# Block 1's attention in two score places: scores of two pairs in three PSUM banks each, turns in pieces through one bank, heads copied by VectorE

## The chip, the cores and the metric

One core of a Trainium2 chip runs the whole program. The metric is the device time in microseconds (us) of one execution; the number given is the median of several. TensorE (PE) multiplies, VectorE (DVE) and ScalarE (ACT) work on what it leaves in PSUM, GpSimd (POOL) works on SBUF, SyncE (SP) starts the weight transfers. PSUM has eight banks of 512 float32 columns; BANK = 512 in the code. Each engine executes its own instructions in order and waits on semaphores for the others.

## The reference

Two transformer blocks run one after the other on 512 tokens of width 1024, each with two layers. The change touches only the attention of the first block. It has eight windowed heads with a sink logit (branch A, at most 384 near keys and 256 context keys) and eight full heads (branch B, all 512 + 256 keys):

```python
s_win = jnp.where(valid[None, :, None, None], s_win, NEG_INF)
s_ctx = jnp.einsum('bnqhgd,bchd->bnhgqc', qb, kc).astype(jnp.float32) * scale
p = softmax_with_sink(jnp.concatenate([s_win, s_ctx], axis=-1), sink.reshape(N_KV_A, G)).astype(v.dtype)
...
s = jnp.einsum('bqhgd,bkhd->bhgqk', qblk, kall).astype(jnp.float32) * scale
p = jax.nn.softmax(s, axis=-1).astype(vall.dtype)
return jnp.einsum('bhgqk,bkhd->bqhd', p, vall)
```

In layer 0 the 256 context tokens attend as well, each to the 256 context keys, in both branches (`context_attention`). Both blocks go on with projections and a gated MLP; all is float32.

## The kernel before

The program is a row of stages, each an `nc.Block()` with one instruction stream per engine; a stage begins when all engines have left the one before. Most of the time goes into matrix products in which each weight is split into a high part (ACT, line 456) and a low part (DVE, line 459). Block 1's attention is one such stage per layer: layer 0 from about 290 to 482 us, layer 1 from about 1375 to 1535 us. Most of the rest is the same before and after the change.

An attention stage walks over *pairs*: two heads (e = 0 and 1) of one tile of 128 queries. Head 0 uses the first 64 rows of TensorE, head 1 the last 64, so that the score products of both run side by side. `pairs1(l)` makes the list. For each of four head pairs and each of four query tiles stands first a windowed pair (branch A: 512, 640, 640, 512 keys for the four tiles, with a mask and a sink), then a full pair (branch B: 768 keys). That makes 32 pairs. Layer 0 adds 16 small pairs for the context tokens, of 256 keys, with and without sink in turn. In this text A512, A640 and B name the three large kinds, and "small" the fourth; a *group* is the eight pairs of one head pair, A512 B A640 B A640 B A512 B.

A pair takes these steps. The letters are those of the prediction:

- S, `scores` (PE, line 1533): the scores of both heads into PSUM.
- M, `maxima` (DVE, lines 1589 to 1597): for each head the mask (in place) and the row maximum, then a scaled copy of it, one 128x1 instruction.
- E, `exponent` (ACT, line 1636): exp into `probs`, one instruction per head; for a pair with sink two more of 128x1 (line 1643).
- N, `normalize` (DVE, lines 1605 to 1609): the reciprocal of the sums, and one multiplication per head over all keys.
- T, `turn` (PE, line 1549): transposes of `probs` into PSUM, 128x128 at a time.
- C, `copy` (ACT, line 1627): the transposed tiles back into `probs`.
- V, `values` (PE, line 1562): the product with the values, into the PSUM place `O_AT`.
- H, `heads` (ACT, line 1648): that result to SBUF; POOL then splits it (lines 1680 and 1681).

What sets the order is the code of the four loops. In turn i of the loop PE does S(i), T(i-1), V(i-2); DVE does N(i-1), M(i); ACT does E(i), C(i-1), H(i-2). A large pair of scores has one place in PSUM, banks 0 and 1 for head 0 and banks 2 and 3 for head 1, so S(i) waits for both E(i-1) (`clear_of`). Where two pairs in a row have at most 512 keys there are two places, and `begun` lets S and M run one pair ahead: PE then does S(i+1) before T(i-1). T has three banks, one after the other for the heads (`T_AT`). The last turns also split the first two weight units of the next stage (`split_unit`, one instruction of 128x1024 on ACT and one on DVE each).

## Time and profile before

| | us |
|---|---|
| median of 3 runs | 3474.71 (3474.41 to 3478.57) |
| the profiled execution | 3481.14 |
| its span, first to last instruction | 3479.2 |
| PE busy | 3310.0 (95%) |
| DVE busy | 1807.0 (52%) |
| ACT busy | 1210.4 (35%) |
| mean granted TensorE clock | 0.988 of 2.4 GHz |

The two attention stages together take about 350 us of the span. Busy time of PE counts the modelled ends of its matmuls, about 0.2 us of tail after the last one of a burst, so a PE that looks almost busy can still have room. A float32 matmul shows as two records in the trace, and a transpose as one. "Idle before" in a row is how long the engine stood before that instruction, and the name after the arrow is what it waited for.

### The profile page before, as it was taken

What the parts mean: (1) busy time and instruction counts of PE and PEld (TensorE: products, weight loads), DVE (VectorE), ACT (ScalarE), POOL (GpSimd) and SP (SyncE); (2) the same over time, 40 slices, a digit from 0 to 9 for tenths busy, and PEclk for the clock granted to TensorE, in tenths of its full rate; (3) what the DMA queues carried; (4) which work ended last, traced back from release to release, by engine and by line L of the source; (5) the groups of instructions that cost most, each with busy time, mean ns of one, the idle gap of its engine ahead of it and who ended that gap; (6) DMA issues with size and microseconds to landing.
All of it is one profiled execution on the core that took longest, in us unless ns stands there. A gap on an engine that the chain in (4) does not pass through costs nothing. (4 is left out here: it accounts for less than half of the span.)

```text
span 3479.2 us, 49806 instructions
## 1 busy us (share of the span) xinstructions
PE 3310.0 (95%) x20432; PEld 2653.7 (76%) x20432; DVE 1807.0 (52%) x2942; ACT 1210.4 (35%) x2054; POOL 445.8 (13%) x477
## 2 busy tenths in 40 slices
PE   6998899999999999889999999899999998899998
PEld 4887678788888787666787867667888777578886
DVE  5875767654232466765323357664443385734433
ACT  3214763311131222763223333353322332533322
POOL 0211111000000021113600133120000022200000
PEclk9999999999999999999999999999999999999999
DMA  6420013354212122012222321012223320022232
GB/s 241 146 103 14 1 45 130 120 197 146 65 63 73 49 86 72 1 37 88 97 92 96 103 85 62 20 43 91 97 91 103 103 85 3 31 91 97 91 102 80
DMA packets 78266, 290.67 MB, mean 84 GB/s; under 512 B 8672, under 2 KB 9056, under 8 KB 77280
## 3 DMA queue, kind: packets, MB, share of 16 engines
q1 hardware_dynamic: 78048, 287.55, 24.3%
q8 instruction: 163, 2.67, 0.3%
q14 instruction: 55, 0.45, 0.0%
HBM read 285.42 MB, written 2.10 MB: 83 GB/s over the span
## 5 line engine op out<-in xcount | busy, mean ns | idle before, releaser
L459 DVE TENSOR_TENSOR w_low<-ring,w_high 128x1024 fp32r<-128x1024 f32 x418 | 526.8, 1260 | 1350.8 <-ACT w_high L456 1350.1
L494 PE MATMUL ps<-arena_r,w_high 128*128 128x512 f32 x3568 | 1143.8, 386 | 10.4 <-PEq L1515 9.1
L456 ACT ACTIVATE w_high<-ring 128x1024 fp32r<-128x1024 f32 x418 | 442.9, 1060 | 1517.6 <-PE ps L494 1508.5
L494 PEld LDWEIGHTS ps<-arena_r,w_high 128*128 128x128 f32 x3568 | 646.8, 188 | 163.6 <-issue 16.9
L494 PE MATMUL ps<-low,w_high 128*128 128x512 f32 (+1 forms) x2448 | 765.2, 361 | 0.0
L494 PE MATMUL ps<-high,w_high 128*128 128x512 f32 x2368 | 737.1, 362 | 15.1 <-DVE low L992 6.9
L494 PE MATMUL ps<-high,w_low 128*128 128x512 f32 x2368 | 730.9, 359 | 0.0
L494 PE MATMUL ps<-arena_r,w_low 128*128 128x512 f32 (+1 forms) x1456 | 546.3, 388 | 0.0
L494 PEld LDWEIGHTS ps<-low,w_high 128*128 128x128 f32 x2448 | 412.1, 189 | 74.9 <-issue 1.2
L494 PEld LDWEIGHTS ps<-high,w_high 128*128 128x128 f32 x2368 | 395.4, 189 | 95.4 <-issue 12.0
L494 PEld LDWEIGHTS ps<-high,w_low 128*128 128x128 f32 x2368 | 395.1, 188 | 70.5
L494 PEld LDWEIGHTS ps<-arena_r,w_low 128*128 128x128 f32 x1456 | 267.1, 189 | 61.6
L555 POOL TENSOR_TENSOR tmp<-tmp 128x512 f32<-128x512 f32 (+1 forms) x42 | 67.3, 1603 | 1528.8 <-ACT tmp L545 1528.8
L1636 ACT ACTIVATE probs<-ps,stat 128x512 f32<-128x512 f32 (+3 forms) x224 | 153.6, 692 | 92.3 <-DVE stat L1594 46.8
L1533 PE MATMUL ps<-arena 64*128 64x256 f32 (+6 forms) x784 | 143.3, 438 | 44.4 <-ACT probs L1636 38.4
L1533 PEld LDWEIGHTS ps<-arena 64*128 64x128 f32 (+1 forms) x784 | 83.1, 193 | 87.3 <-ACT probs L1636 54.0
L1549 PE MATMUL ps<-const,probs 128*128 128x128 f32 x896 | 126.5, 285 | 17.9 <-DVE probs L1609 8.9
L1549 PEld LDWEIGHTS ps<-const,probs 128*128 128x128 f32 x896 | 100.8, 144 | 54.3 <-DVE probs L1609 42.0
L802 DVE CUSTOM_DVE_ANT_0 arena<-arena 128x1024 f32<-128x1024 f32 x104 | 137.1, 1362 | 0.0
L1627 ACT ACTIVATE probs<-ps 128x512 f32<-128x512 f32 (+3 forms) x224 | 121.1, 597 | 24.4 <-PE ps L1549 23.5
L494 PE MATMUL ps<-low,w_low 128*128 128x512 f32 x368 | 127.4, 374 | 0.0
L1562 PE MATMUL ps<-probs,arena 128*64 128x128 f32 x1792 | 123.5, 280 | 2.8 <-ACT hL L1648 2.2
(353 smaller groups left out, 2941.4 us busy)
## 6 DMA issues: line engine op xcount, KB each, us to landing
ring<-in_weights SPq DMA_DIRECT2D x428, 512.0 KB, 3.3
arena<-in_ada_rows SPq DMA_DIRECT2D x80, 512.0 KB, 3.9
arena<-in_ada SPq DMA_DIRECT2D x16, 512.0 KB, 15.7
arena<-in_cond_rows SPq DMA_DIRECT2D x3, 1024.0 KB, 5.9
xL<-in_x SPq DMA_DIRECT2D x1, 2048.0 KB, 10.4
out<-xL SPq DMA_DIRECT2D x4, 512.0 KB, 2.7
low_f<-in_low_rank SPq DMA_DIRECT2D x3, 512.0 KB, 4.3
const<-in_const SPq DMA_DIRECT2D x1, 1104.0 KB, 5.4
```

Of the source, the lines that this page charges most:

```text
L456: act.activation(w_high[:, slot, :], ring[:, place, :], ACT.Copy).then_inc(unit_high.sem, 1)
L459: dve.tensor_tensor(w_low[:, slot, :], ring[:, place, :], w_high[:, slot, :].bitcast(F32), ALU.subtract).then_inc(unit_free.sem, 1)
L494: mm = pe.matmul(bank(4 * (t % 2) + 2 * p + s, width), w, g.split[k][s][x], start=(n == 0 and m == 0), stop=(n == len(part) - 1 and m == 2))
L555: pool.tensor_tensor(tmp[:, 1, 0:total], tmp[:, 1, 0:total], tmp[:, 0, 0:total], ALU.add).then_inc(squares_sum.sem, 1)
L802: ins = dve.tensor_tensor_reduce(out, self.slots[place], self.vectors[s], 1.0, 0.0, ALU.mult, ALU.add, mod[:, to, s:s + 1])
L1533: mm = pe.matmul(ps[:, to:to + w], q, k, start=True, stop=True)
L1549: mm = pe.transpose(ps[:, to:to + P], probs[:, j % 3, e, m * P:m * P + P], con("ident"))
L1562: mm = pe.matmul(ps[e * HD:e * HD + HD, O_AT:O_AT + P], pair["values"][e][m], probs[:, j % 3, e, m * P:m * P + P], start=(m == 0 and not b ...
L1627: act.activation(probs[:, j % 3, e, 0:keys], ps[:, turned_at(j, e):turned_at(j, e) + keys], ACT.Copy).then_inc(turned_out.sem, 1)
L1636: act.activation(probs[:, i % 3, e, 0:keys], ps[:, scores_at(i, e):scores_at(i, e) + keys], ACT.Exp, bias=st[:, 2 + e:3 + e], scale=scale, ...
```

## The change

A second function, `attention_by_bank`, is added and is used for block 1 in both layers; `attention` stays for block 2. Six things differ from the function before:

- Scores have two places for every kind of pair: banks 0 to 2 and banks 3 to 5, in turn. A large pair has head 0 in the first bank and half of the second, head 1 in the other half and the third. S(i) waits for E(i-2).
- The middle bank of a large pair is shared by both heads. Head 1 writes it first and head 0 last, and between the two PE waits on its own semaphore (`shared_bank`). For B, head 1's scores are cut at 256 and not at 512, so the order is 512 (head 0), 256 (head 1), 512 (head 1), wait, 256 (head 0).
- The probabilities of both heads stand one behind the other, and T and C go through one bank (bank 6) in pieces of up to 512 columns: B and A640 have three pieces, A512 two, a small pair one. Each piece waits until the piece before it is copied.
- The order within a turn i of the loop is new. PE: T(i-1) piece 0, S(i+1), T(i-1) piece 1, V(i-2), T(i-1) piece 2. DVE: N(i-1), H(i-3), M(i+1). ACT: E(i) head 0, C(i-1) piece 0, E(i) head 1, C(i-1) piece 1, sinks, C(i-1) piece 2.
- H is done by DVE (`tensor_copy`), after N and before M, and in the last turns after the two `split_unit`.
- E of a large pair waits for the maxima of both heads.

```diff
+        shared_bank = count("shared_bank")
...
+        def attention_by_bank(pairs, scale, heads_on_vector=False):
+            n = len(pairs)
+            T_AT, O_AT = 6 * BANK, 7 * BANK
+            chunks = [-(-2 * pair["keys"] // BANK) for pair in pairs]
+            chunk0 = [sum(chunks[:i]) for i in range(n + 1)]
+            def scores_at(i, e):
+                return (i % 2) * 3 * BANK + e * (T if pairs[i]["keys"] > BANK else BANK)
...
+            def chunk(i, c):
+                return c * BANK, min((c + 1) * BANK, 2 * pairs[i]["keys"])
+                    def scores(i):
+                        pair = pairs[i]
+                        if i >= 2:
+                            pe.wait_ge(exp_out.sem, exp_out.at(2 * (i - 2) + 2))
+                        for c in range(len(pair["scores"][0])):
+                            for f in ((0, 1) if c % 2 == 0 else (1, 0)):
+                                q, k, at, w = pair["scores"][f][c]
+                                to = scores_at(i, f) + at
+                                shared = pair["keys"] > BANK and (f, c) == (0, len(pair["scores"][0]) - 1)
+                                if shared:
+                                    pe.wait_ge(shared_bank.sem, shared_bank.at(large(i + 1)))
+                                mm = pe.matmul(ps[:, to:to + w], q, k, start=True, stop=True)
+                                if pair["keys"] > BANK and (f, c) == (1, 0):
+                                    mm.then_inc(shared_bank.sem, 1)
+                        mm.then_inc(scores_in.sem, 2)
+                    def turn(j, c):
+                        first, end = chunk(j, c)
+                        pe.wait_ge(probs_out.sem, probs_out.at(2 * j + (1 if end <= pairs[j]["keys"] else 2)))
+                        if chunk0[j] + c:
+                            pe.wait_ge(turned_out.sem, turned_out.at(chunk0[j] + c))
+                        for at in range(first, end, P):
+                            to = T_AT + at - first
+                            mm = pe.transpose(ps[:, to:to + P], flat(j)[:, at:at + P], con("ident"))
+                        mm.then_inc(turned_in.sem, 1)
+                    def values(j):
+                        pair = pairs[j]
+                        pe.wait_ge(turned_out.sem, turned_out.at(chunk0[j + 1]))
+                        if j:
+                            pe.wait_ge(heads_copied.sem, heads_copied.at(j))
+                        tiles = pair["keys"] // P
+                        for m in range(tiles):
+                            for e in range(2):
+                                mm = pe.matmul(ps[e * HD:e * HD + HD, O_AT:O_AT + P], pair["values"][e][m],
+                                               of_head(j, e)[:, m * P:m * P + P], start=(m == 0), stop=(m == tiles - 1))
+                        mm.then_inc(heads_in.sem, 1)
+                    scores(0)
+                    scores(1)
+                    for i in range(1, n + 2):
+                        j = i - 1
+                        if j < n:
+                            turn(j, 0)
+                        if i + 1 < n:
+                            scores(i + 1)
+                        if j < n and chunks[j] > 1:
+                            turn(j, 1)
+                        if j >= 1:
+                            values(j - 1)
+                        if j < n and chunks[j] > 2:
+                            turn(j, 2)
...
+                    def maxima(i):
+                        pair = pairs[i]
+                        st, keys = stat[:, 8 * (i % 4):8 * (i % 4) + 8], pair["keys"]
+                        dve.wait_ge(scores_in.sem, scores_in.at(2 * i + 2))
+                        for e in range(2):
+                            part = ps[:, scores_at(i, e):scores_at(i, e) + keys]
...
+                    def normalize(j):
+                        pair, st = pairs[j], stat[:, 8 * (j % 4):8 * (j % 4) + 8]
...
+                    def heads(j):
+                        dve.wait_ge(heads_in.sem, heads_in.at(j + 1))
+                        dve.tensor_copy(pairs[j]["y"], ps[:, O_AT:O_AT + P]).then_inc(heads_copied.sem, 1)
+                    maxima(0)
+                    for i in range(n + 3):
+                        if 0 <= i - 1 < n:
+                            normalize(i - 1)
+                        if heads_on_vector and i >= 3:
+                            heads(i - 3)
+                        if i == n:
+                            split_unit(None, dve, 0, 0, None, 0)
+                            split_unit(None, dve, 1, 1, None, 0)
+                        if i + 1 < n:
+                            maxima(i + 1)
+                    def copy(j, c):
+                        first, end = chunk(j, c)
+                        act.wait_ge(turned_in.sem, turned_in.at(chunk0[j] + c + 1))
+                        act.activation(flat(j)[:, first:end], ps[:, T_AT:T_AT + end - first], ACT.Copy).then_inc(turned_out.sem, 1)
+                    def exponent(i, e):
+                        pair, st = pairs[i], stat[:, 8 * (i % 4):8 * (i % 4) + 8]
+                        act.wait_ge(max_out.sem, max_out.at(2 * i + (2 if pair["keys"] > BANK else e + 1)))
+                        if i >= 3:
+                            act.wait_ge(heads_in.sem, heads_in.at(i - 2))
+                        act.activation(of_head(i, e), ps[:, scores_at(i, e):scores_at(i, e) + pair["keys"]],
+                                       ACT.Exp, bias=st[:, 2 + e:3 + e], scale=scale,
+                                       accum_out=st[:, 4 + e:5 + e]).then_inc(exp_out.sem, 1)
...
+                    for i in range(n + 2):
+                        j = i - 1
+                        if i < n:
+                            exponent(i, 0)
+                        if 0 <= j < n:
+                            copy(j, 0)
+                        if i < n:
+                            exponent(i, 1)
+                        if i == n:
+                            split_unit(act, None, 0, 0, None, 0)
+                        if 0 <= j < n and chunks[j] > 1:
+                            copy(j, 1)
+                        if i < n and pairs[i]["sink"] is not None:
+                            sink(i)
+                        if i >= 2 and not heads_on_vector:
+                            heads(i - 2)
+                        if 0 <= j < n and chunks[j] > 2:
+                            copy(j, 2)
+                        if i == n:
+                            split_unit(act, None, 1, 1, None, 0)
...
-                    pairs.append({"scores": [[(z[r, Z_QB + pair, n * P:n * P + P], z[r, Z_KB, 0:S], 0, S),
-                                              (z[r, Z_QB + pair, n * P:n * P + P], z[r, Z_KB, S:T], S, C)] for r in halves],
+                    pairs.append({"scores": [[(z[r, Z_QB + pair, n * P:n * P + P], z[r, Z_KB, a:b], a, b - a) for a, b in parts]
+                                             for r, parts in zip(halves, (((0, S), (S, T)), ((0, C), (C, T))))],
-            attention(pairs1(l), HD ** -0.5)
+            attention_by_bank(pairs1(l), HD ** -0.5, True)
```

How the rows of the program move, at two places. The first is PE in the middle of layer 0's large pairs. Line 1533 (1744 in the new kernel) is S, 1549 (1756) is T, 1562 (1767) is V. Before, from the V of an A640 on, through one B and the T of the A640 ahead of it:

```order
L1562 MATMUL ps<-probs,arena 64x128 [waits heads_copied,turned_out]
L1562 MATMUL ps<-probs,arena 64x128 x9
L1533 MATMUL ps<-arena 128x512 [waits exp_out]
L1533 MATMUL ps<-arena 128x512
L1533 MATMUL ps<-arena 128x256 x2
L1549 MATMUL ps<-const,probs 128x128 [waits turned_out,probs_out]
L1549 MATMUL ps<-const,probs 128x128 x4
L1549 MATMUL ps<-const,probs 128x128 [waits turned_out,probs_out]
L1549 MATMUL ps<-const,probs 128x128 x4
```

Now, PE in the new kernel at the same kind of place, one turn of its loop and the first piece of the next:

```order
L1756 MATMUL ps<-const,probs 128x128 [waits turned_out,probs_out]
L1756 MATMUL ps<-const,probs 128x128 x3
L1744 MATMUL ps<-arena 128x512 [waits exp_out]
L1744 MATMUL ps<-arena 128x256
L1744 MATMUL ps<-arena 128x512
L1744 MATMUL ps<-arena 128x256 [waits shared_bank]
L1756 MATMUL ps<-const,probs 128x128 [waits turned_out,probs_out]
L1756 MATMUL ps<-const,probs 128x128 x3
L1767 MATMUL ps<-probs,arena 64x128 [waits heads_copied,turned_out]
L1767 MATMUL ps<-probs,arena 64x128 x9
L1756 MATMUL ps<-const,probs 128x128 [waits turned_out,probs_out]
L1756 MATMUL ps<-const,probs 128x128 x3
```

Before, the scores of a pair stand ahead of the turns and wait for exponentials alone. Now the first piece of turns, which waits for N (`probs_out`), stands ahead of the scores, and these are of the pair after the next.

The second place is DVE in the large pairs. Line 1606 (1812 in the new kernel) and 1609 (1815) are N, 1592 and 1597 (1798 and 1803) are M of a B. Before, N of an A640 (its last three instructions), M of a B, and N of that B:

```order
L1606 RECIPROCAL stat<-stat 128x2 [waits chain_v]
L1609 TENSOR_SCALAR probs<-probs,stat 128x640 [waits chain_v]
L1609 TENSOR_SCALAR probs<-probs,stat 128x640
L1592 TENSOR_REDUCE stat<-ps 128x1 [waits scores_in]
L1597 TENSOR_SCALAR stat<-stat 128x1 [waits chain_v]
L1592 TENSOR_REDUCE stat<-ps 128x1 [waits scores_in]
L1597 TENSOR_SCALAR stat<-stat 128x1 [waits chain_v]
L1606 RECIPROCAL stat<-stat 128x2 [waits exp_out]
```

Now, DVE: N of a B, H of an earlier pair (line 1819), M of the B after it, and N of the A640 that lies between the two:

```order
L1812 RECIPROCAL stat<-stat 128x2 [waits exp_out]
L1815 TENSOR_SCALAR probs<-probs,stat 128x768 [waits chain_v]
L1815 TENSOR_SCALAR probs<-probs,stat 128x768
L1819 COPY hL<-ps 128x128 [waits heads_in]
L1798 TENSOR_REDUCE stat<-ps 128x1 [waits scores_in]
L1803 TENSOR_SCALAR stat<-stat 128x1 [waits chain_v]
L1798 TENSOR_REDUCE stat<-ps 128x1
L1803 TENSOR_SCALAR stat<-stat 128x1 [waits chain_v]
L1811 TENSOR_TENSOR stat<-stat 128x2 [waits sinks_out,exp_out]
```

In both kernels N and M alternate on DVE. Before, the M behind N(i-1) is that of pair i (for small pairs, of i+1); now it is that of pair i+1 everywhere, with a copy of heads ahead of it.

## Rows read from the trace of the kernel before

**Rows 1.** Windows: one group of large pairs (layer 0), then the small pairs.

```profile
core 0: us, PE busy (x) PEld busy (x) DVE busy (x) ACT busy (x) POOL busy (x), PEclk, DMA share, GB/s
333.17:370.53 37.36, 32.19 (x330) 25.27 (x329) 26.50 (x69) 27.32 (x64) 6.06 (x16) 1.00 0.01 2
445.08:476.39 31.31, 29.57 (x264) 17.97 (x262) 28.17 (x115) 29.78 (x123) 10.99 (x30) 1.00 0.01 2
```

**Rows 2.** Timeline, large pairs: start, us, engine, line, operation, count, [idle before <- releaser].

```profile
400.67 0.33 PEld L1533 LDWEIGHTS ps<-arena 64*128 64x128 f32 x4 [0.33 <-ACT probs L1636]
400.70 1.56 PE L1533 MATMUL ps<-arena 64*128 64x512 f32 x8
401.43 0.88 DVE L1609 TENSOR_SCALAR probs<-probs,stat 128x512 f32<-128x512 f32 x2
402.30 0.96 DVE L1592 TENSOR_REDUCE stat<-ps 128x1 f32<-128x768 f32 x1
402.44 0.86 PEld L1549 LDWEIGHTS ps<-const,probs 128*128 128x128 f32 x8 [0.58 <-DVE probs L1609]
403.30 0.15 DVE L1597 TENSOR_SCALAR stat<-stat 128x1 f32<-128x1 f32 x1
403.37 0.95 DVE L1592 TENSOR_REDUCE stat<-ps 128x1 f32<-128x768 f32 x1
404.54 0.90 ACT L1636 ACTIVATE probs<-ps,stat 128x768 f32<-128x768 f32 x1
405.68 1.15 PE L1533 MATMUL ps<-arena 64*128 64x128 f32 x12 [0.68 <-ACT probs L1636]
406.86 0.70 DVE L1589 CUSTOM_DVE_ANT_0 ps<-ps,const 128x512 f32<-128x512 f32 x1
408.81 0.69 ACT L1636 ACTIVATE probs<-ps,stat 128x512 f32<-128x512 f32 x1
409.74 1.56 PE L1533 MATMUL ps<-arena 64*128 64x512 f32 x8 [0.43 <-ACT probs L1636]
```

**Rows 3.** Timeline, the scores of an A640.

```profile
386.99 1.36 PE L1533 MATMUL ps<-arena 64*128 64x256 f32 x12 [0.51 <-ACT probs L1636]
```

**Rows 4.** Instruction groups by form, large pairs: count | busy us, mean ns of one.

```profile
L1609 DVE TENSOR_SCALAR probs<-probs,stat 128x768 f32<-128x768 f32 x8 | 4.6, 618 | 0.1
L1609 DVE TENSOR_SCALAR probs<-probs,stat 128x640 f32<-128x640 f32 x4 | 2.0, 550 | 0.1
L1589 DVE CUSTOM_DVE_ANT_0 ps<-ps,const 128x640 f32<-128x640 f32 x4 | 3.3, 827 | 0.3 <-PE ps L1533 0.3
```

**Rows 5.** Timeline, small pairs of layer 0.

```profile
450.80 0.66 PE L1549 MATMUL ps<-const,probs 128*128 128x128 f32 x4
450.91 0.42 DVE L1592 TENSOR_REDUCE stat<-ps 128x1 f32<-128x256 f32 x1 [0.99 <-PE ps L1533]
451.38 0.66 PE L1562 MATMUL ps<-probs,arena 128*64 128x128 f32 x8
451.97 0.70 PE L1533 MATMUL ps<-arena 64*128 64x256 f32 x4
451.97 0.16 DVE L1605 TENSOR_TENSOR stat<-stat 128x2 f32<-128x2 f32 x1
452.37 0.68 DVE L1609 TENSOR_SCALAR probs<-probs,stat 128x256 f32<-128x256 f32 x2
452.41 0.51 ACT L1636 ACTIVATE probs<-ps,stat 128x256 f32<-128x256 f32 x1
475.94 0.51 ACT L1636 ACTIVATE probs<-ps,stat 128x256 f32<-128x256 f32 x1
```

**Rows 6.** The page's costliest groups, whole span: VectorE's half of a weight split.

```profile
L459 DVE TENSOR_TENSOR w_low<-ring,w_high 128x1024 fp32r<-128x1024 f32 x418 | 526.8, 1260 | 1350.8 <-ACT w_high L456 1350.1
```

**Rows 7.** Windows and timeline at the start of layer 0's attention.

```profile
290.00:295.00 5.00, 1.81 (x14) 1.52 (x16) 2.16 (x8) 3.21 (x7) 0.00 (x0) 0.81 0.00 0
297.19 1.97 PE L1549 MATMUL ps<-const,probs 128*128 128x128 f32 x8
```

More of the change, by code:

```diff
@@ L1695, in attention, with sinks, large, flat @@
                 c.base += m * n
+        shared_bank = count("shared_bank")
[6 more added lines that the diff above has]
+                return (i % 2) * 3 * BANK + e * (T if pairs[i]["keys"] > BANK else BANK)
+            def sinks(i):
+                return sum(pair["sink"] is not None for pair in pairs[:i])
+            def large(i):
+                return sum(pair["keys"] > BANK for pair in pairs[:i])
+            def flat(i):
+                return probs[:, i % 3].rearrange("p e t -> p (e t)")
+            def of_head(i, e):
+                return flat(i)[:, e * pairs[i]["keys"]:(e + 1) * pairs[i]["keys"]]
+            def chunk(i, c):
+                return c * BANK, min((c + 1) * BANK, 2 * pairs[i]["keys"])
+            with nc.Block() as block:
+                @block.tensor
+                def _(pe):
+                    def scores(i):
[47 more added lines that the diff above has]
+                            turn(j, 2)
+                @block.vector
+                def _(dve):
+                    def maxima(i):
[4 more added lines that the diff above has]
+                            part = ps[:, scores_at(i, e):scores_at(i, e) + keys]
+                            if pair["mask"] is not None:
+                                chain_v.link(dve, dve.tensor_tensor_reduce(
+                                    part, part, pair["mask"], 1.0, -3e38, ALU.add, ALU.max, st[:, e:e + 1]))
+                            else:
+                                chain_v.link(dve, dve.tensor_reduce(st[:, e:e + 1], part, AX_X, ALU.max))
+                            if pair["sink"] is not None:
+                                dve.tensor_scalar(st[:, 2 + e:3 + e], st[:, e:e + 1], -scale, pair["sink"][e][1],
+                                                  ALU.mult, ALU.min).then_inc(max_out.sem, 1)
+                            else:
+                                dve.tensor_scalar(st[:, 2 + e:3 + e], st[:, e:e + 1], -scale, None,
+                                                  ALU.mult).then_inc(max_out.sem, 1)
+                    def normalize(j):
+                        pair, st = pairs[j], stat[:, 8 * (j % 4):8 * (j % 4) + 8]
+                        dve.wait_ge(exp_out.sem, exp_out.at(2 * j + 2))
+                        if pair["sink"] is not None:
+                            dve.wait_ge(sinks_out.sem, sinks_out.at(sinks(j + 1)))
+                            chain_v.link(dve, dve.tensor_tensor(st[:, 4:6], st[:, 4:6], st[:, 6:8], ALU.add))
+                        chain_v.link(dve, dve.reciprocal(st[:, 4:6], st[:, 4:6]))
+                        for e in range(2):
+                            p = of_head(j, e)
+                            dve.tensor_scalar(p, p, st[:, 4 + e:5 + e], None, ALU.mult).then_inc(probs_out.sem, 1)
+                    def heads(j):
[12 more added lines that the diff above has]
+                            maxima(i + 1)
+                @block.scalar
+                def _(act):
+                    def copy(j, c):
[10 more added lines that the diff above has]
+                                       accum_out=st[:, 4 + e:5 + e]).then_inc(exp_out.sem, 1)
+                    def sink(i):
+                        pair, st = pairs[i], stat[:, 8 * (i % 4):8 * (i % 4) + 8]
+                        for e in range(2):
+                            ins = act.activation(st[:, 6 + e:7 + e], pair["sink"][e][0], ACT.Exp, bias=st[:, 2 + e:3 + e])
+                        ins.then_inc(sinks_out.sem, 1)
+                    def heads(j):
+                        act.wait_ge(heads_in.sem, heads_in.at(j + 1))
+                        act.activation(pairs[j]["y"], ps[:, O_AT:O_AT + P], ACT.Copy).then_inc(heads_copied.sem, 1)
+                    for i in range(n + 2):
[18 more added lines that the diff above has]
+                            split_unit(act, None, 1, 1, None, 0)
+                @block.gpsimd
+                def _(pool):
+                    for j, pair in enumerate(pairs):
+                        y, (hi, lo) = pair["y"], pair["halves"]
+                        pool.wait_ge(heads_copied.sem, heads_copied.at(j + 1))
+                        chain_g.link(pool, pool.tensor_copy(hi, y))
+                        pool.tensor_tensor(lo, y, hi.bitcast(F32), ALU.subtract)
+            heads_copied.base += n
+            sinks_out.base += sinks(n)
+            shared_bank.base += large(n)
+            turned_in.base += chunk0[n]
+            turned_out.base += chunk0[n]
+            for c, m in ((scores_in, 2), (max_out, 2), (exp_out, 2), (probs_out, 2), (heads_in, 1)):
+                c.base += m * n
```

## The prediction

> **What bounds the attention now.** I read the windows first, then the timeline of two pairs, then the groups by form. One group of eight large pairs lasts 37.36 us, and in it no engine is full: PE is busy for 32.19 us, ACT for 27.32, DVE for 26.50 [rows 1]. So a loop of waits sets the pace, and the timeline names it: the scores of a B (400.70) begin when the exponentials before them have ended, DVE's reduction begins 0.04 us after the scores (400.70 + 1.56 = 402.26, then 402.30), the exponential of the second head at 404.54 when the second maximum is there, the next scores at 405.68 after "ACT probs L1636", and so on to 409.74 [rows 2]. That is E, S, M, E: 9.04 us for an A512 and a B. T, V, N, C and H all lie beside it. The small pairs are another thing: they have two places, S and M run one pair ahead, and ACT is busy for 29.78 of 31.31 us and DVE for 28.17 [rows 1]. Their pace is (475.94 - 452.41) / 12 = 1.96 us a pair [rows 5].
>
> **What the change does to the loop.** Two places take E out of the loop: S(i+1) waits for E(i-1), which is long past. Taken alone that would free the stage down to its busiest engine. But the new order makes another loop. On PE, S(i+1) stands behind T(i-1) piece 0. That piece waits for N(i-1) on DVE. On DVE, M(i+1) waits for S(i+1), and N(i) stands behind M(i+1). So each turn must hold, one after the other: N(i-1) of the first head, T piece 0, S(i+1), M(i+1). Before, N and T were beside the loop. Each pair pays this once; nothing can be issued round it, since both engines go in order.
>
> **Its terms.** N up to the first head's end: the two 128x2 steps of a pair with sink take 452.37 - 451.97 = 0.40 [rows 5], so one takes 0.20. A512: 0.40 + 0.44 (half of 0.88) = 0.84 [rows 2]; A640: 0.40 + 0.55 = 0.95; B, without sink: 0.20 + 0.62 = 0.82 [rows 4]. DVE to PE: 401.43 + 0.88 = 402.31, weights of the turn at 402.44, so 0.13 [rows 2]. A piece of four transposes up to the start of what follows it: 451.38 - 450.80 = 0.58 [rows 5]. S: A512 1.15 [rows 2], A640 1.36 [rows 3]. S to M: 0.04. M of a B: 402.30 to 404.50, less the 0.08 by which the instruction after a small one overlaps it (403.37 against 403.30 + 0.15), 2.12; of an A512: 406.86 to 408.78, less 0.08, 1.84 [rows 2]; of an A640 two times 0.827 - 0.70 more, 2.10 [rows 4].
>
> S of a B in its new cut has no row. Each head still streams 768 columns, so it isn't under today's 1.56; with no work side by side it would be twice that less one tail of 0.2, 2.9. I take 1.70, near the lower end: the two heads still overlap, but a piece of 512 now runs beside one of 256, and the last 256 waits on a semaphore that head 1's first 256 has given while head 0's 512 still streams. Each 0.1 us here costs 32 x 0.1 = 3.2 us in all.
>
> The Trainium skill ("TensorE: Matmul & The Clock Gate", section "Step-by-step: what each phase is for") says that matmuls stay in program order and only weight loads are pulled ahead. By that rule head 0's last 256 can't begin before head 1's 512 has, and S of a B would be nearer 1.9, the sum some 6 us higher; the eight records in 1.56 us [rows 2] show the heads side by side but not this order of widths.
>
> **Large pairs.** A turn with a B: 0.82 + 0.13 + 0.58 + 1.70 + 0.04 + 2.12 = 5.39. The four A turns of a group: N 2 x 0.84 + 2 x 0.95 = 3.58, joints 4 x 0.75 = 3.00, S 2 x 1.15 + 2 x 1.36 = 5.02, M 2 x 1.84 + 2 x 2.10 = 7.88, together 19.48. Group: 4 x 5.39 + 19.48 = 41.0 against 37.36, +3.7. There are 4 groups in each of 2 layers: +29 us. With S of a B at 1.56 it would be +25, at 2.9 it would be +68.
>
> Does anything else exceed these turns? PE's own work stays about 32 us of 41, 78%. The pieces form a chain too, T 0.66 [rows 5], C, which I estimate at 0.6 since an exponential over the same 512 columns takes 0.69 [rows 2], and a wait of 0.13: 1.4 a piece, three of them 4.2, beside turns of 5.2 to 5.4. The last copy of an A640 comes close to the next turn's first piece, within about 0.1 us, so I leave a few us for it in the range. H on DVE lies in the 2 us in which DVE waits for the scores; its price I bound by a 128x1 instruction, 0.15, and half a 128x768 reduction, 0.48. Both fit, so it costs nothing here, and what it frees on ACT was not needed.
>
> **Small pairs.** The same loop, with both heads of N ahead of the single piece: N 0.40 + 0.68 = 1.08 with sink, 0.88 without, mean 0.98; then 0.13, 0.58, S 0.70, 0.04, M 451.97 - 450.91 = 1.06 [rows 5]. Sum 3.49 against 1.96, +1.53 for each of 16 pairs in layer 0: +24.5 us. Here the engines had been full, so the second place was there already and only the loss remains.
>
> **Start and end of the stages.** In the last turns the heads' copies stand behind both weight splits on DVE, 1.26 us each [rows 6], and the last V waits for the copy before it. Before, the second split ran beside that V. I count one split and one V of a B, 1.26 + 1.5 (eight records take 0.66, so 24 take 3 x 0.46 + 0.2 [rows 5]), about 3 us a layer, 6 in all; 0 to 10 is possible. What the two first M before the first N cost (under 1 us) and what the last turns save without an M cancel.
>
> **Sum.** 29 + 24.5 + 6 = 60 us. The profiled execution took 3481.1, 6.4 above the median of 3474.7, and would become 3541; on the median it is 3535. In percent +1.7; about 0.2% is what a measurement of this kernel tells from no change.
>
> **Rivals.**
>
> *The clock falls in the small pairs.* PE's records of a small pair are 0.66 + 0.70 + 0.66 = 2.0 us [rows 5], 58% of 3.49, where before PE was busy for 94% [rows 1]. At the start of layer 0 a window with PE busy 36% was granted 0.81, and right behind it eight transposes took 1.97 us, where 2 x 0.46 + 0.2 = 1.1 is their time at 2.4 GHz: that is 1.2 GHz [rows 7]. A fall would add about 0.43 to T and 0.5 to S of every small pair, 15 us: 3550. Against it: the gaps are short and even, and with T, S and V twice as long PE would be busier again.
>
> The Trainium skill ("TensorE: Matmul & The Clock Gate", section "Part 4: PE-mode transpose") says that transposes don't count as busy for the gate in the way other matmuls do. By that the counted share of a small pair would be 1.36 of 3.49, 39%, which speaks for this rival; the small pairs before would have had 69%, and kept 1.00 [rows 1], so the trace neither bears out nor denies it.
>
> *Scores one after the other.* If the wait on `shared_bank` or the new cut takes most of the overlap away, S of a B is 2.2 to 2.9 and that of an A640 rises too: 16 to 39 us more, 3551 to 3574.
>
> *Faster: the busiest engine sets the pace.* If the new loop had enough slack (if S(i+1) got out before N(i-1) ended), the group would fall to PE's 32.2 us, 5.2 us less, 41 us in all, and the small pairs would stay: about 3434. It decides from the point where N + T + S + M is under PE's work, about 4.0 us a pair; it is 4.6 to 5.4. Speaks for it: PE did stand still for 5 us a group. Against it: M alone is 1.8 to 2.1 and S 1.2 to 1.7, and both are in the turn whatever the rest does.
>
> *No change* would need the large pairs to win what the small lose, 25 us, so a turn of 3.9 us.
>
> **Chances.** The forecast (3512 to 3549) 0.72; the clock 0.15; scores one after the other 0.07; faster 0.04; no change 0.02. So slower by over 0.2%: 0.94, within 0.2%: 0.02, faster: 0.04. Range: its lower end is the sum without the end term, with S of a B at 1.56 and some 12 us for overlaps that the joints don't show, 3512; the upper end takes in the clock rival and part of the next, 3562.
>
> **What would show it.** In the new trace DVE should wait in nearly every turn for "PE ps L1744" ahead of M, about 1.6 us at a B (from the end of H to the end of the scores) and about 1.1 us at a small pair, and PE's T piece 0 for "DVE probs L1815"; a group should last 41 us and a small pair 3.5; ACT should hardly wait for maxima longer than before. S of a B should read 1.6 to 1.8. The copies of heads should stand inside DVE's gap. If instead PE is busy throughout and groups last 33 us, the loop isn't what I say. If the clock in the small pairs reads 0.5 to 0.9, the first rival has it.

## The result, and the profile after

The changed kernel takes 3543.07 us (median of 4 runs, 3539.18 to 3550.22) against 3476.64 us for the kernel before (median of 4, 3474.41 to 3481.52). The ratio is 1.0191, with a 95% interval of 1.0171 to 1.0212: about 66 us slower. The forecast was 3535, in a range of 3512 to 3562. The profiled execution took 3539.18 us, 58.1 more than that of before (3481.1), where the forecast's sum was 60.

The windows first: core time, then busy time (and records) of each engine, the granted clock, DMA. The first stretch is one group of large pairs, the others run from the small pairs into the next stage.

```profile
412.92:454.70 41.78, 35.52 (x330) 25.36 (x329) 27.69 (x77) 27.07 (x62) 5.95 (x16) 1.00 0.01 2
470.00:510.00 40.00, 22.51 (x192) 13.63 (x192) 24.33 (x99) 20.37 (x71) 8.92 (x24) 1.00 0.00 1
510.00:520.00 10.00, 3.87 (x29) 2.76 (x31) 5.04 (x14) 4.09 (x9) 1.95 (x6) 0.68 0.00 0
520.00:530.00 10.00, 8.14 (x38) 6.77 (x36) 0.29 (x1) 0.00 (x0) 1.03 (x3) 0.64 0.56 209
```

A group lasts 41.8 us instead of 37.36 [rows 1], with the same work on DVE and ACT but for H, 2.3 us a group, which has moved from ACT to DVE. PE's busy time grew by 3.3 us. The two heads' scores of a B now take 1.96 us instead of 1.56 [rows 2], 1.6 us in four turns. Most of the rest lies in the transposes, which now end in 22 pieces a group, each with its own tail: counted alone they are busy for 14.3 us instead of 11.2, part of it beside other matmuls. In the small pairs no engine is near full any more, where ACT had been busy for 29.78 of 31.31 us [rows 1].

The timeline shows a turn with a B: start, us, engine, line, operation, count, idle time before and its releaser.

```profile
417.54 0.15 DVE L1812 RECIPROCAL stat<-stat 128x2 f32<-128x2 f32 x1
418.41 0.66 PE L1756 MATMUL ps<-const,probs 128*128 128x128 f32 x4 [0.70 <-DVE probs L1815]
418.99 1.96 PE L1744 MATMUL ps<-arena 64*128 64x512 f32 x8
420.98 0.96 DVE L1798 TENSOR_REDUCE stat<-ps 128x1 f32<-128x768 f32 x1 [1.91 <-PE ps L1744]
423.11 0.16 DVE L1811 TENSOR_TENSOR stat<-stat 128x2 f32<-128x2 f32 x1
```

It reads as one chain without a gap: N from 417.54, T piece 0 at 418.41, S at 418.99, M at 420.98, the next N at 423.11. That is 0.87 + 0.58 + 1.99 + 2.13 = 5.57 us. Three of the four B turns of a group last that long. In the fourth, T piece 0 waits for something else:

```profile
407.16 0.15 DVE L1812 RECIPROCAL stat<-stat 128x2 f32<-128x2 f32 x1
407.35 1.15 DVE L1815 TENSOR_SCALAR probs<-probs,stat 128x768 f32<-128x768 f32 x2
407.72 0.38 ACT L1838 ACTIVATE probs<-ps 128x256 f32<-128x256 f32 x1 [1.23 <-PE ps L1756]
408.25 0.63 PE L1756 MATMUL ps<-const,probs 128*128 128x128 f32 x4 [0.56 <-ACT probs L1838]
408.41 0.29 DVE L1819 COPY hL<-ps 128x128 f32<-128x128 f32 x1
408.80 1.96 PE L1744 MATMUL ps<-arena 64*128 64x512 f32 x8
410.80 0.96 DVE L1798 TENSOR_REDUCE stat<-ps 128x1 f32<-128x768 f32 x1 [2.10 <-PE ps L1744]
412.92 0.16 DVE L1811 TENSOR_TENSOR stat<-stat 128x2 f32<-128x2 f32 x1
```

The first head's N was done by 407.97, but ACT's copy of the third piece of the pair before ended only at 408.10, and the first piece goes into the same bank. So this turn is 1.09 + 0.55 + 2.00 + 2.12 = 5.76 us. In a group T piece 0 waits for N in six turns and for that copy in two, which costs 0.2 us here and under 0.1 in the other (an A512). DVE stands still for 2.10 us, and H (0.29) lies just ahead of that, between N and M, at no cost. Before, at a turn with a B, DVE's reduction followed the scores by 0.04 us as well, but the scores had waited for an exponential [rows 2]; now the exponentials end unseen, and N and T stand in the way.

The waits of the small pairs (470 to 510 us: engine and line, what it waited for, us in total, times, longest):

```profile
PE ps L1756 <- DVE probs L1815: 18.5, 12, 1.6
ACT probs L1838 <- PE ps L1756: 18.3, 12, 1.6
DVE stat L1798 <- PE ps L1744: 14.3, 12, 1.2
```

There are 12 of each in 12 pairs: every turn of every pair waits once on PE for N, once on ACT for T, once on DVE for S. The timeline of one of these pairs:

```profile
484.13 0.66 PE L1756 MATMUL ps<-const,probs 128*128 128x128 f32 x4 [1.59 <-DVE probs L1815]
484.71 0.70 PE L1744 MATMUL ps<-arena 64*128 64x256 f32 x4
485.46 0.42 DVE L1798 TENSOR_REDUCE stat<-ps 128x1 f32<-128x256 f32 x1 [1.19 <-PE ps L1744]
486.63 0.15 DVE L1812 RECIPROCAL stat<-stat 128x2 f32<-128x2 f32 x1
487.49 0.65 PE L1756 MATMUL ps<-const,probs 128*128 128x128 f32 x4 [1.49 <-DVE probs L1815]
```

From one T to the next it is 3.36 us here; the mean of 12 pairs is 3.415, against 1.96 before [rows 5].

Where the 58 us lie, from first and last N of each stage in the two profiles:

| | forecast | profile |
|---|---|---|
| 64 large pairs | +29 | +30.8 (layer 0 15.8, layer 1 15.0) |
| small pairs and the step into them | +24.5 | +20.5 |
| last N to the next stage's first matmul | +6 | +8.1 (6.1 to 9.3, 7.7 to 12.6) |

The three rows of the profile add up to 59.4; the other stages together are 1.3 us shorter.

### The profile page after: what moved, and what is told of

It reads as the page before. It is cut to its first block and busy times, and to the rows that moved or that the text cites. A ratio compares the mean times of both kernels' runs of the same rounds, so it can differ in the third digit from the quotient of the medians.

```text
span 3537.3 us, 49826 instructions
## 1 busy us (share of the span) xinstructions
PE 3333.2 (94%) x20432; PEld 2653.3 (75%) x20432; DVE 1819.4 (51%) x3022; ACT 1205.5 (34%) x2006; POOL 442.6 (13%) x477
## 5 line engine op out<-in xcount | busy, mean ns | idle before, releaser
L1756 PEld LDWEIGHTS ps<-const,probs 128*128 128x128 f32 x736 | 78.5, 143 | 124.3 <-DVE probs L1815 97.4
L1838 ACT ACTIVATE probs<-ps 128x512 f32<-128x512 f32 x192 | 111.2, 579 | 131.0 <-PE ps L1756 127.5
L1845 ACT ACTIVATE probs<-ps,stat 128x768 f32<-128x768 f32 (+3 forms) x160 | 119.4, 746 | 21.5 <-DVE stat L1800 11.7
L1744 PE MATMUL ps<-arena 64*128 64x256 f32 (+2 forms) x672 | 117.7, 440 | 2.1 <-PEq L1289 2.1
L1798 DVE TENSOR_REDUCE stat<-ps 128x1 f32<-128x768 f32 (+1 forms) x96 | 74.4, 775 | 80.5 <-PE ps L1744 80.5
L1767 PE MATMUL ps<-probs,arena 128*64 128x128 f32 x1472 | 100.2, 282 | 6.4 <-DVE hC L1819 3.3
```

Of the source, the lines that this page charges most:

```text
L1744: mm = pe.matmul(ps[:, to:to + w], q, k, start=True, stop=True)
L1756: mm = pe.transpose(ps[:, to:to + P], flat(j)[:, at:at + P], con("ident"))
L1767: mm = pe.matmul(ps[e * HD:e * HD + HD, O_AT:O_AT + P], pair["values"][e][m], of_head(j, e)[:, m * P:m * P + P], start=(m == 0), stop=(m = ...
L1798: chain_v.link(dve, dve.tensor_reduce(st[:, e:e + 1], part, AX_X, ALU.max))
L1838: act.activation(flat(j)[:, first:end], ps[:, T_AT:T_AT + end - first], ACT.Copy).then_inc(turned_out.sem, 1)
L1845: act.activation(of_head(i, e), ps[:, scores_at(i, e):scores_at(i, e) + pair["keys"]], ACT.Exp, bias=st[:, 2 + e:3 + e], scale=scale, accu ...
```

## The experiments

Each median stands beside that of the kernel before in its own session, 3477.5 to 3478.9. "Group" is the length of eight large pairs in the profile, "small" the pace of the small pairs. PE's queue in the changed kernel, on which the edits are made, holds T(i-1) piece 0, S(i+1), T piece 1, V(i-2), T piece 2.

**1 and 2. The scores ahead of the turn.** On PE, in the first for all pairs, in the second for the small ones alone:

```
+ if i + 1 < n: scores(i + 1)        # second: only if keys < BANK
  turn(j, 0)
- if i + 1 < n: scores(i + 1)
```

> The changed kernel with one edit: on PE the scores S(i+1) stand ahead of the first piece of turns T(i-1). My theory (the loop N, T, S, M sets the pace): the loop is gone, DVE hardly waits for scores any more, and PE's own work sets the large pairs, three pieces 1.74 + V 1.46 + S 1.9 = 5.1 us for a B, 4.0 for an A640, 3.2 for an A512, a group of about 35 us instead of 41.6; a small pair falls from 3.4 to about 2.3 us (DVE's own work). Sum 8 x 6.6 + 16 x 1.1 = about 70 us less than the changed kernel, 3473 us (3462 to 3490). Rival one (the pieces through one bank and the waits for their copies set the pace) and rival two (the wait on the shared bank does): the order of S and T changes little, 3530 us or more.

> The changed kernel, S(i+1) ahead of T(i-1) only where pair i+1 is a small one (256 keys). My theory gives back the small pairs' part alone: 16 x 1.1 = 18 us, 3525 us (3519 to 3530), the large groups stay at 41.6 us. If the small pairs were slow because the heads' copy fills DVE, or because a piece waits for both heads' probabilities, they would stay at 3.4 us and the time at 3543.

First: 3528.04 (3527.17 to 3532.47), ratio 1.0145 [1.0128, 1.0162]; group 41.67, small 2.97. Second: 3540.57 (3537.28 to 3545.27), 1.0177 [1.016, 1.0194]; group 41.83, small 2.97. Both gained far less than expected; the first came out where its rivals had put it, at about 3530. Its 15 us came from the small pairs (6.3) and from the large pairs of the two layers (4.6 and 3.9), nearly all in the first group of each stage, where the pipeline fills. The later groups hardly moved, from 41.84 to 41.67, and the timeline of the first says why (the third and fourth rows are ACT's copy of piece 0 and the exponential behind it):

```profile
403.24 1.96 PE L1744 MATMUL ps<-arena 64*128 64x512 f32 x8
405.12 0.66 PE L1756 MATMUL ps<-const,probs 128*128 128x128 f32 x4
405.82 0.60 ACT L1841 ACTIVATE probs<-ps 128x512 f32<-128x512 f32 x1 [1.42 <-PE ps L1756]
406.31 0.68 ACT L1848 ACTIVATE probs<-ps,stat 128x512 f32<-128x512 f32 x1
406.56 0.63 PE L1756 MATMUL ps<-const,probs 128*128 128x128 f32 x4 [0.78 <-ACT probs L1841]
407.12 1.31 PE L1767 MATMUL ps<-probs,arena 128*64 128x128 f32 x20
408.36 0.66 PE L1756 MATMUL ps<-const,probs 128*128 128x128 f32 x4
```

The scores run early, but piece 1 goes into the bank that piece 0's copy must empty first. S had covered that copy; now PE stands still for 0.78 us. A third loop shows: PE's own order with its uncovered copies. In the small pairs yet another holds, over ACT:

```profile
480.43 0.66 PE L1756 MATMUL ps<-const,probs 128*128 128x128 f32 x4
481.12 0.60 ACT L1841 ACTIVATE probs<-ps 128x512 f32<-128x512 f32 x1 [1.14 <-PE ps L1756]
481.62 0.47 ACT L1848 ACTIVATE probs<-ps,stat 128x256 f32<-128x256 f32 x1
482.06 0.47 ACT L1855 ACTIVATE stat<-small,stat 128x1 f32<-128x1 f32 x2
482.64 0.16 DVE L1814 TENSOR_TENSOR stat<-stat 128x2 f32<-128x2 f32 x1 [1.03 <-ACT stat L1855]
483.71 0.66 PE L1756 MATMUL ps<-const,probs 128*128 128x128 f32 x4 [0.78 <-DVE probs L1818]
```

T, C, the second head's E, which stands behind C on ACT, then N and T again. So there are three loops: (1) N, T, S, M; (2) T, C, E, N; (3) PE's order.

**3 and 4. The heads back on ACT, two pairs behind**, alone and with edit 1:

```
- attention_by_bank(pairs1(l), HD ** -0.5, True)
+ attention_by_bank(pairs1(l), HD ** -0.5, False)
```

> The changed kernel with the heads copied by ScalarE, two pairs behind, instead of by VectorE. My theory: the copy on VectorE lies in the time in which it waits for scores, so nothing changes in the loop, and only the ends of the stages gain 2 to 5 us: 3540 us (3536 to 3544). Rival (VectorE has become the bound through the 80 copies): 80 x 0.29 = 23 us less, 3520.

> Both edits: scores ahead of the first piece of turns, heads copied by ScalarE. My theory: the large pairs are at PE's own work and don't change against scores-first alone; the small pairs, then bound by VectorE, gain up to 0.28 us each, 4 us, and the ends some 3 us: 3466 us (3455 to 3480). Rival (ScalarE is the next bound in the small pairs, as before the change): no gain over scores-first alone.

Alone: 3548.71 (3544.38 to 3557.26), 1.0197 [1.018, 1.0214]; group 42.45, small 3.69 where the clock was full. Both: 3528.67 (3526.15 to 3530.51), 1.0143 [1.0126, 1.016], group 41.66, the same as edit 1; 3466 had been expected. Alone, the ends gained what was expected: in the profile they were 1.6 and 3.7 us shorter (7.7 and 8.9 us instead of 9.3 and 12.6). But each group lost 0.6 us and each small pair 0.28: H on ACT waits for V and holds the next pair's exponential behind it.

```profile
485.00 0.28 ACT L1857 ACTIVATE hC<-ps 128x128 f32<-128x128 f32 x1 [0.18 <-PE ps L1767]
485.17 0.47 ACT L1845 ACTIVATE probs<-ps,stat 128x256 f32<-128x256 f32 x1
```

So the move of H to DVE cost some 5 us at the ends and gave back somewhat more within the stages; it is no large part of the loss. The difference of the two whole kernels is within their intervals; only the lengths in the profiles show these shares.

**5 and 6. The exponentials ahead of the copies**, in the fifth with edit 1, in the sixth alone. On ACT:

```
+ exponent(i, 0); exponent(i, 1)
  copy(j, 0)
- exponent(i, 0); ...; exponent(i, 1)
```

> Scores ahead of the first piece of turns on PE, and on ACT both heads' exponentials ahead of the first copy. After the first four runs my theory is that there are three loops of nearly one length: (1) N, T piece 0, S, M; (2) T piece 0, its copy C, the second head's E behind that copy, N; (3) for large pairs PE itself, S, T, T, V, T with one copy of 0.78 us that nothing covers. Scores-first broke (1) and uncovered the first copy, so large groups stayed at 41.7 us by (3), small pairs stopped at 2.97 by (2). This edit breaks (2) as well: small pairs go to VectorE's own work, 2.3 to 2.4 us, 16 x 0.6 = 10 us less than scores-first; groups stay at 41 to 41.7. 3518 us (3512 to 3524). Rival (small pairs are held by the waits between PE and VectorE, N and T, whatever ACT does): they stay at 2.97 and the time at 3528.

> The changed kernel with only ACT's order edited: both heads' exponentials ahead of the first copy. My theory: loop (1) is untouched, so small pairs stay at 3.4 us and groups at 41.8: 3543 us (3539 to 3546). Rival (loop (2) alone explains the small pairs): they fall to 2.5 to 3.0, 3530.

Fifth: 3540.85 (3537.52 to 3542.23), 1.0177 [1.016, 1.0194], where 3518 was expected. The small pace was 2.45, as loop (2) demanded, but the group was 43.60, longer than the 41 to 41.7 expected: now the copy waits behind two exponentials and PE for the copy.

```profile
406.03 0.90 ACT L1848 ACTIVATE probs<-ps,stat 128x768 f32<-128x768 f32 x1
406.91 0.60 ACT L1841 ACTIVATE probs<-ps 128x512 f32<-128x512 f32 x1
407.66 0.63 PE L1756 MATMUL ps<-const,probs 128*128 128x128 f32 x4 [1.38 <-ACT probs L1841]
```

Sixth: 3552.24 (3546.74 to 3558.24), 1.0208 [1.0191, 1.0225], where at most 3546 was expected; group 42.53, 0.7 more than expected, nearly all of it in one B turn, 6.36 instead of 5.76, where T piece 0 waits for the copy. Where the clock was full its small pairs kept the changed kernel's pace, 3.41: with S still behind T, loop (1) holds there in spite of ACT's new order. The groups account for some 5.5 of the 9 us lost; I put the rest down to the clock, below, which one profile suggests and no run separates.

**7. The values in two halves around the second piece**, on top of edit 5, so that each copy has half of V beside it (where the pair being turned has only two pieces, all of V stands ahead of the second):

```
+ values(j - 1, 0)
  turn(j, 1)
- values(j - 1)
+ values(j - 1, 1)
  turn(j, 2)
```

> As scores-and-exponentials-first, and where a pair has three pieces, V of the pair before is cut in two and stands between the pieces: S, T, first half of V, T, second half of V, T. Every copy then has matmuls beside it. My theory: loops (1) to (3) are all gone, PE's own work is 34.9 us a group and the halves of V cover all but some 0.15 us of each copy, so a group takes 36 to 38 us, a small pair 2.35: 3543 - 8 x 5 - 16 x 1.05 = 3486 us (3476 to 3498), about the kernel before. Rival (the pieces' chain through one bank, 22 pieces a group, sets the pace whatever stands between): groups of 40 us or more, 3510 or more.

3497.01 (3494.39 to 3499.68), 1.0057 [1.004, 1.0074]; group 38.47, small 2.45. 46 of the 66 us are back, with the same work and the same places in PSUM. The time lies at the upper edge of what was expected (3486, up to 3498), the group 0.5 us above it.

```profile
407.71 0.66 PE L1756 MATMUL ps<-const,probs 128*128 128x128 f32 x4
408.30 0.66 PE L1769 MATMUL ps<-probs,arena 128*64 128x128 f32 x8
409.14 0.63 PE L1756 MATMUL ps<-const,probs 128*128 128x128 f32 x4 [0.19 <-ACT probs L1845]
```

PE waits 0.19 us for the copy instead of 0.78.

**8 and 9. Work added to the changed kernel beside loop (1), and work moved into it.** The eighth does the second piece's transposes twice in the large pairs (0.5 us each, some 31 us in all, off the loop). The ninth adds nothing; it puts H (0.29 us) ahead of N on DVE:

```
  mm = pe.transpose(...)        # eighth, inside turn(j, 1)
+ mm = pe.transpose(...)        # the same once more
---
+ heads(i - 3)        # ninth
  normalize(i - 1)
- heads(i - 3)
```

> The changed kernel with the second piece of turns of every large pair done twice (the same transposes to the same place, 64 pairs x about 0.49 us on PE = 31 us of added PE work, none in the small pairs). This piece isn't in loop (1). If (1) alone sets the pace of the large pairs, PE has about 0.7 us of room a pair and the time stays within 5 us of 3543. If PE's own loop (3) is nearly as long, as I now think, most of it shows at the B turns: +15 to +28 us, 3558 to 3571.

> The changed kernel with VectorE's copy of heads moved from behind N to ahead of it: no work is added, 0.29 us moves from the wait for scores into loop (1) (N, T piece 0, S, M). If loop (1) binds, each of 80 turns grows by 0.29 us and more where the copy has to wait for V: groups from 41.8 to 44.1 or more, small pairs from 3.41 to 3.70, +23 us, 3566 (3558 to 3578). If VectorE's total work or PE's own loop binds instead, nothing changes: 3543.

Eighth: 3562.05 (3552.17 to 3580.22), 1.0251 [1.0214, 1.0288]; group 44.02, so 2.2 of the 3.9 us added to a group came through. Two of the four B turns stayed at 5.57; the other six turns of the group grew by 0.2 to 0.4 us each. In five of those six T piece 0 now waits for the third piece's copy: PE's own order, with this copy that nothing covers, was already within 0.3 us of loop (1). An A512 turn of this run shows it:

```profile
420.54 0.63 PE L1756 MATMUL ps<-const,probs 128*128 128x128 f32 x4 [0.78 <-ACT probs L1840]
```

Ninth: 3578.98 (3574.32 to 3583.03), 1.0293 [1.0277, 1.0309]; group 43.67, +1.83, or 0.23 us a turn (the three B turns bound by loop (1) alone all grew by just that, 5.57 to 5.80; the others by 0.04 to 0.40). An instruction of 0.29 us that was free behind N costs most of its length ahead of it: loop (1) is real. In the small pairs with the clock at 1.00 the cost was more, 0.4 to 0.5 us, because H there also waits for V (0.67 and 0.21 us in two turns that I looked at), so they are no clean test. The whole kernel lost 36 us where 23 were expected; part of the rest is half clock in the small pairs (490 to 520):

```profile
490.00:520.00 30.00, 20.84 (x101) 12.17 (x100) 14.11 (x51) 11.45 (x38) 4.70 (x12) 0.50 0.00 1
```

**10. B's scores in equal cuts**, three of 256 for both heads instead of 512 + 256 beside 256 + 512:

```
- for r, parts in zip(halves, (((0, S), (S, T)), ((0, C), (C, T))))
+ for r, parts in zip(halves, 2 * (((0, C), (C, S), (S, T)),))
```

> The changed kernel with the scores of a B cut into three pieces of 256 for both heads (as an A640 is), so that pieces of one width run side by side; three banks and the shared-bank wait stay. My theory: S of a B fell behind (1.96 us in the profile against 1.56 before) because a piece of 512 stood beside one of 256; with equal pieces it is 1.5 to 1.65, both the loop and PE's own work get 0.35 us shorter at 32 B: -11 us, 3532 (3526 to 3537), groups 40.4. Rival (the wait on the shared bank costs the 0.4 us): S stays at 1.9 or more and the time at 3543.

3533.16 (3525.78 to 3534.42), 1.0155 [1.014, 1.0171]; group 40.32.

```profile
395.88 0.66 PE L1756 MATMUL ps<-const,probs 128*128 128x128 f32 x4 [0.60 <-DVE probs L1815]
396.46 1.57 PE L1744 MATMUL ps<-arena 64*128 64x256 f32 x12
```

S of a B takes 1.57 us, what it took before the change [rows 2], though the wait on `shared_bank` is still there. So the 0.4 us came with the unequal widths and not with that wait alone. Single records of the changed kernel's trace agree: at the B of 408.80 the matmul that gives the semaphore ended at 409.51, and the piece that waits for it began only at 410.09. The B turns fell by 0.38 us each, 5.57 to 5.19 and 5.76 to 5.38.

**11 and 12. All edits together, and the ends.** The twelfth moves the two weight splits on DVE behind the last copies of heads; the eleventh is edits 7, 10 and 12.

```
- if i == n: both splits
+ if i == n + 1: split 0      # behind heads(i - 3)
+ if i == n + 2: split 1
```

> The values-in-halves kernel (scores first, both exponentials ahead of the first copy, V cut around the second piece) with the equal pieces of scores and with VectorE's two weight splits moved behind the last copies of heads. Theory: 3497 less 8 to 11 for the scores and 4 to 5 for the ends: 3483 us (3476 to 3490), groups 37.0 to 37.4, small pairs still 2.45 against 1.97 before, so no faster than the kernel before (3478).

> The changed kernel with VectorE's two weight splits moved behind the copies of heads in the last turns. Theory: from the last N to the next stage it took 9.3 us against 6.1 before in layer 0; 2.3 us come back in each layer: 3538.5 us (3536 to 3542), hard to tell from 3543 by the time, read from the trace. Rival (the stage's end was set by ScalarE's splits): no change in that stretch.

Twelfth: 3544.21 (3543.54 to 3551.14), 1.02 [1.0185, 1.0216]: not told apart from the changed kernel as a whole, though in the profile the end of layer 0 shortened from 9.3 to 7.4 us and that of layer 1 from 12.6 to 9.8, about what was expected. Eleventh: 3480.78 (3477.84 to 3482.24, 11 runs) against 3477.47 (15 runs), 1.0007 [0.9998, 1.0016]: no change from the kernel before, as expected.

```profile
332.79:369.69 36.90, 34.83 (x346) 25.69 (x345) 27.97 (x76) 26.49 (x62) 5.97 (x16) 1.00 0.01 2
```

Its groups are 0.5 us shorter than before's 37.36, PE busy for 94% of them, and the first group of each stage is 2.4 and 3.3 us shorter. From first to last N, the large pairs of the two profiles give back 3.8 us in layer 0 and 6.0 in layer 1. Its small pairs take 2.45 against 1.96, with the step into them 5.8 us more, and its ends are 3.9 us longer. So -9.8, +5.8 and +3.9 cancel, as the medians say. No version tried beats the kernel before.

## Why the prediction was right

**The mechanism.** N, T piece 0, S, M in nearly every turn, across two engines that go in order: the timeline shows the chain without a gap, the waits show it 12 times in 12 small pairs, the ninth experiment adds to it and pays, and the second takes it out of the small pairs, which fall from 3.42 to 2.97. The tenth takes from it and gains, but S stands in PE's own order as well, so that run can't tell the two apart. ACT's waits for maxima came down, as said: in a group they were 5.5 + 4.1 us before and are 1.0 now (second row; engine and line, what was waited for, us in total, times, longest).

```profile
ACT probs L1838 <- PE ps L1756: 12.3, 16, 1.2
ACT probs L1845 <- DVE stat L1800: 1.0, 1, 1.0
```

The exponential that bound the kernel before is out of the loop, as the change means it to be, and what took its place is longer.

**Large pairs.** The group was to be 41.0 and is 41.8. A B turn was to be 5.39 and is 5.57, once in a group 5.76; the four A turns were to be 19.48 and are 19.37 (5.03 + 5.10 + 4.62 + 4.62, each within 0.1 of its own sum). The term that was mis-sized is S of a B, taken at 1.70, measured 1.96, outside the 1.6 to 1.8 that I had named as a sign. I took the value near today's 1.56 because eight records ran side by side in it; with the new widths they overlap less. N and its joint came 0.08 shorter than their sum, which hid a third of it. The Trainium skill ("TensorE: Matmul & The Clock Gate", section "Step-by-step: what each phase is for") has matmuls in program order, from which I had estimated 1.9; the measured 1.96 agrees better with it. The rest is T piece 0 in one B turn of a group, which stood 0.22 us further behind N than in the others, because ACT's copy of the third piece ended late (408.10): the overlap I had left "a few us" for. The eighth experiment shows how close this second path was in most turns.

**Small pairs.** 3.42 a pair against 3.49 forecast, and 20.5 us against 24.5. The 12 pairs in the middle cost 12 x (3.415 - 1.966) = 17.4; the other four, with the step from the large pairs, cost 3.1 where the forecast had 6.1. N with its joint was taken too long, 1.21 and 1.01 with and without sink where 1.07 and 0.86 were measured, and M a little too short. The edges of a stage don't pay in full.

**Ends.** Forecast 6 us with 0 to 10 possible, measured 8.1. The cause was as said: the last copies stand behind the splits.

```profile
516.83 2.36 DVE L459 TENSOR_TENSOR w_low<-ring,w_high 128x1024 fp32r<-128x1024 f32 x2 [2.58 <-ACT w_high L456]
519.11 0.28 DVE L1819 COPY hC<-ps 128x128 f32<-128x128 f32 x1
519.54 1.12 PE L1767 MATMUL ps<-probs,arena 128*64 128x128 f32 x8 [3.27 <-DVE hC L1819]
1592.10 2.81 PE L1767 MATMUL ps<-probs,arena 128*64 128x128 f32 x24 [3.18 <-DVE hL L1819]
```

PE stands still for over 3 us, and then works at 1.2 GHz (granted 0.51 from 1592.10 to 1594.90, 1.00 in the 4 us before): the last V of layer 1, 24 records, took 2.81 us where I had reckoned 1.5. That is 1.3 of the 2.1 us above forecast. Layer 0's last V has only 8 records and took 1.12 us, where 8 records took 0.66 before [rows 5].

**The rival of the clock.** In this profile the small pairs kept 1.00 for 40 us. In those of the third, fourth, sixth, ninth and tenth experiments part of them ran at 0.50, and the changed kernel's runs differ by 11 us in the order of their mean clock (3539.18 at 0.989, 3550.22 at 0.985). So it is not a rival but an addition, present in some executions. I take it for the reason why the medians lie 66 apart and the profiles 58; of the other runs only the mean clock shows, so that stays argued.

**Luck.** That the profile's 58 us lie so near the forecast's 60 is in part luck: the large pairs cost 1.8 more than forecast, the small ones 4 less, the ends 2.1 more, and the other stages were 1.3 shorter.

**The faster rival** said that a group would fall to PE's 32.2 us if S got out before N. The first experiment made just that condition true and the group stayed at 41.67. Its premise was too simple, and so was my sentence that PE's own 32 us fit beside the loop: behind loop (1) stood two others of nearly the same length. With all three opened the group fell to 38.5 (7), and with the equal cuts besides to 36.9 (11).

**No change.** One sum of the prediction is off: to win 25 us in 64 large pairs each turn must be 0.4 us shorter than today's 4.67, so 4.3 us and not 3.9. Nothing else was worked out from it.

## What to carry to other kernels

A second buffer takes a wait away only if nothing that stands ahead of the buffered work in its engine's queue depends on the previous item: here S(i+1) had its own place but stood behind a transpose that waited for N(i-1). Before moving work, write down each engine's order for one turn and follow every closed path through two or three of them, with what covers each copy; the shortest edit that opens one loop can uncover the next, so edits must be judged together (1 gained 15 us, 5 gained 2, 7 gained 46). Where a copy must end before the next piece may begin, put part of an independent group of matmuls into each such gap.

## What the runs showed of the hardware

- Scores of two heads side by side ran faster in equal widths: 2 x 768 columns took 1.96 us as 8 records of 512 beside 256, 1.57 as 12 records of 256 beside 256, and 1.56 before the change as 512 beside 512 and 256 beside 256.
- The granted clock in the small pairs was not settled by their pace. In the changed kernel it held 1.00 for 40 us with PE busy for 22.51 of them. In the tenth experiment it was 0.50 in the first stretch below, though PE was busy for 15.70 of 20 us, and 1.00 again from 500 us on, with PE busy for 5.43 of 10. I had expected a stage of one pace to have one clock; what decides between the two is open.

```profile
470.00:490.00 20.00, 15.70 (x78) 9.20 (x78) 8.88 (x36) 8.61 (x29) 3.51 (x10) 0.50 0.00 1
500.00:510.00 10.00, 5.43 (x49) 3.38 (x48) 6.27 (x25) 5.10 (x17) 2.11 (x6) 1.00 0.00 1
```

- A clock that falls at the end of a thin stage is paid for by the next, which begins at 522.52: from 520 to 530 the granted clock was 0.64, with PE busy for 8.14 us.
